# Twenty-eight products ahead of the first transposes, and the first weight load behind the first token tile, in a one-core hybrid encoder layer

## The reference

```python
def reference(x, w_in, ...):
    u = x @ w_in[l]                       # (1024, 1024) @ (1024, 7688)
    ua, ub, uc, ug = _split(u, GROUP_COLS)
    oa = _gdn_branch(ua, ...)             # gated DeltaNet
    ob, v_first = _rwkv7_branch(ub, ...)  # RWKV-7
    oc = _swa_branch(uc, sinks)           # sliding-window attention
    merged = (gates[:, :, 0] * (oa @ w_branch_a[l]) + gates[:, :, 1] * (ob @ w_branch_b[l])
              + gates[:, :, 2] * (oc @ w_branch_c[l]))
    x = _layer_norm(ALPHA * x + merged @ w_out[l], ln1_w[l], ln1_b[l])
    hid = jax.nn.silu(x @ ffn_gate[l]) * (x @ ffn_up[l])
    x = _layer_norm(ALPHA * x + hid @ ffn_down[l], ln2_w[l], ln2_b[l])
    return x
```

## Time and profile before

| what | us |
|---|---|
| median of three runs | 1816.58 |
| span of the profiled execution | 1816.2 |
| PE busy in it | 1781.5 (98%) |
| first transpose on PE | 6.35 |
| first product of the projection on PE | 13.42 |

### The profile page before, as it was taken

One profiled execution on the slowest core, in us unless ns is written; L12 is line 12 of the kernel. 1 busy time (PEld: TensorE's weight loads), 2 busy tenths in 40 slices (PEclk: granted clock), 3 DMA queues, 4 the chain that ended last, 5 costly groups with the idle time before them and its releaser, 6 DMA issues. The chain is left out here.

```text
span 1816.2 us, 28096 instructions
## 1 busy us (share of the span) xinstructions
PE 1781.5 (98%) x11148; PEld 1471.3 (81%) x11148; DVE 1141.4 (63%) x1354; ACT 665.2 (37%) x1126; POOL 584.6 (32%) x418
## 2 busy tenths in 40 slices
PE   8999999999999999999999999999999999999997
PEld 7778787777788888788878788888888888888886
DVE  2856665666419930377768854966666665665577
ACT  3534434244421211355542231343333333344341
POOL 1211222212213332344415452755455554500000
PEclk9999999999999999999999999999999999999999
DMA  6255575235673377377665573225545455488464
GB/s 178 50 112 140 141 180 138 65 76 155 166 206 93 93 162 228 126 237 245 186 211 173 163 236 97 101 70 183 171 133 171 143 175 179 139 286 300 169 226 155
DMA packets 386434, 293.24 MB, mean 161 GB/s; under 512 B 172428, under 2 KB 318412, under 8 KB 384256
## 3 DMA queue, kind: packets, MB, share of 16 engines
q1 hardware_dynamic: 310080, 237.63, 44.1%
q10 hardware_dynamic: 76224, 53.81, 10.3%
HBM read 196.33 MB, written 94.98 MB: 160 GB/s over the span
## 5 line engine op out<-in xcount | busy, mean ns | idle before, releaser
L168 PE MATMUL bank<-xhi,w_hi 128*128 128x512 f32 x960 | 379.0, 395 | 2.5 <-ACT turned L847 1.7
L170 PE MATMUL bank<-xhi,w_lo 128*128 128x512 f32 x960 | 374.4, 390 | 0.0
L169 PE MATMUL bank<-xlo,w_hi 128*128 128x512 f32 x960 | 373.8, 389 | 0.0
L472 POOL TENSOR_TENSOR w_lo<-w_raw,w_hi 128x1024 fp32r<-128x1024 f32 x59 | 168.3, 2853 | 538.1 <-ACT w_hi L854 538.1
L168 PEld LDWEIGHTS bank<-xhi,w_hi 128*128 128x128 f32 x960 | 180.3, 188 | 43.3 <-issue 6.8
L170 PEld LDWEIGHTS bank<-xhi,w_lo 128*128 128x128 f32 x960 | 180.2, 188 | 38.4
L169 PEld LDWEIGHTS bank<-xlo,w_hi 128*128 128x128 f32 x960 | 180.4, 188 | 36.1
L2044 POOL TENSOR_TENSOR ff_ring_lo<-ff_w_sums,ff_ring_hi 128x512 fp32r<-128x512 f32 x88 | 125.7, 1430 | 74.6 <-ACT ff_ring_hi L2326 74.4
L2044 POOL TENSOR_TENSOR ff_ring_lo<-ff_raw,ff_ring_hi 128x512 fp32r<-128x512 f32 x66 | 96.2, 1460 | 149.4 <-ACT ff_ring_hi L2326 149.4
L834 ACT ACTIVATE work<-bank 128x512 f32<-128x512 f32 x68 | 40.7, 598 | 244.7 <-PE bank L170 228.4
L175 PE MATMUL b_ps<-x1hi,ff_ring_hi 128*128 128x512 f32 x264 | 102.9, 390 | 0.0
(11 more groups left out here) (418 smaller groups left out, 3968.7 us busy)
## 6 DMA issues: line engine op xcount, KB each, us to landing
w_raw<-in_w_in ACTq DMA_DIRECT2D x61, 512.0 KB, 4.3
hid_ops<-y SPq DMA_DIRECT2D x77, 256.0 KB, 2.8
ff_raw<-hid_ops SPq DMA_DIRECT2D x77, 256.0 KB, 3.9
op<-opnd SPq DMA_DIRECT2D x16, 1152.0 KB, 5.5
u<-work ACTq DMA_DIRECT2D x68, 256.0 KB, 4.3
b_gate<-u SPq DMA_DIRECT2D x24, 512.0 KB, 3.6
ff_raw<-in_ffn_gate SPq DMA_DIRECT2D x22, 512.0 KB, 4.5
ff_raw<-in_ffn_up SPq DMA_DIRECT2D x22, 512.0 KB, 5.7
```

Of the source, the lines that this page charges most:

```text
L168: pe.matmul(out, w_hi, x_hi, start=first, stop=False)
L169: pe.matmul(out, w_hi, x_lo, start=False, stop=False)
L170: return pe.matmul(out, w_lo, x_hi, start=False, stop=last)
L472: pool.tensor_tensor(w_lo[b][:, :, :], w_raw[b][:, :, :], as_f32(w_hi[b][:, :, :]), ALU.subtract).then_inc(w_lo_done, 1)
```

## The change

POOL's first instruction becomes a clearing of 128 columns of slab 17, announced by a semaphore (the former `early_cleared`, renamed `early_zeroed`, whose later wait rises from 4 to 5 for it). PE waits for it and makes 28 products of this piece with itself, 128x128 by 128x128, into the first 128 columns of bank 3, before it waits for the constants; nothing reads the result, and the transposes overwrite it. And ACT waits for `x_landed[0]` before `load_w(0)`.

```diff
+IDLE_PRODUCTS = 28
...
         def _(pool):
+            pool.memset(work[:, 17, 0:P], 0.0).then_inc(early_zeroed, 1)
             pool.wait_ge(w_lo_done, 1)
...
-                pool.memset(inv[b][:, :, :, :], 0.0).then_inc(early_cleared, 1)
-                pool.memset(join[b][:, :, :], 0.0).then_inc(early_cleared, 1)
-            pool.wait_ge(early_cleared, 4)
+                pool.memset(inv[b][:, :, :, :], 0.0).then_inc(early_zeroed, 1)
+                pool.memset(join[b][:, :, :], 0.0).then_inc(early_zeroed, 1)
+            pool.wait_ge(early_zeroed, 5)
...
+            pe.wait_ge(early_zeroed, 1)
+            for _ in range(IDLE_PRODUCTS):
+                pe.matmul(bank[3][:, 0:P], work[:, 17, 0:P], work[:, 17, 0:P], start=True, stop=True)
             pe.wait_ge(const_landed, 16)
             for i in range(4):
                 pe.wait_ge(x_landed[i], 16)
...
+            act.wait_ge(x_landed[0], 16)
             load_w(0)
             split(0)
             load_w(1)
```

More of the change, by code:

```diff
@@ L419, in project_and_prepare @@
         inv_landed, inv_cleared, inv_stored = sem("inv_landed"), sem("inv_cleared"), sem("inv_stored")
-        early_landed, early_inv, early_cleared, early_join, early_placed = (sem("early_" + n) for n in ("landed", "inv", "cleared", "join", "placed"))
+        early_landed, early_inv, early_zeroed, early_join, early_placed = (sem("early_" + n) for n in ("landed", "inv", "zeroed", "join", "placed"))
         inv_step = [sem(f"inv_step{k}") for k in range(2)]
```

## The result

The changed kernel takes 1824.51 us, the median of six runs (1822.39 to 1829.24), against 1816.86 us of the kernel before on the same chips (six runs, 1814.23 to 1820.21). The ratio is 1.0044 with a 95% interval of 1.0032 to 1.0056: slower by 7.7 us (the two medians), with 1823.5 us forecast. The profiled executions differ by as much, 1823.7 against 1816.2 us of span.

A forecast was written before the change was run, and what follows sets the result against it. PE, busy 1781.5 of 1816.2 us, was taken as the bound. A late first product (+4.4 us) and low clock (+2.5) sum to +6.9: span 1823.1, forecast 1823.5 us with the median 0.4 above the span; range 1818.5 to 1827.

The forecast's parts named there:

- The path: At the kernel's start: the first weight load, issued at 4.7 us behind seven queued token tiles, lands about when these drain.
- The working by packets: Queues at the start: token and weight packets alternate, 98 token packets per us, putting the last weights at 14.3 us.
- The landing: First weight tile lands at 14.7 us, some 0.5 us behind its last bytes; bounds 13.5 and 17.
- From landing to product: From the weight tile's landing through split, lo part and first `xlo` to PE's first product: 3.15 us.
- The late first product: PE's first product starts at 17.85 us instead of 13.42: +4.4 us, bounds +3.2 and +6.7.
- The clock: After about 8 us idle, PE's first products run at the low clock: +2.5 us, bounds 1.6 and 3.2.
- The 28 products: At PE's start: they take 3.1 to 6.0 us, end between 4.2 and 7.1, and raise the clock for the transposes.
- A: Rival: weight load takes its median 4.3 us and lands at 9.0; 1815.4 us, or 1817.0 with low clock; chance 0.15.
- B: Rival: weights land late, but the clock stays up or later PE waits shrink; +3.5 us, 1820.1; chance 0.13.
- C: Rival: weights come early enough that tokens decide, first product 2.9 us sooner; 1813.7 us; chance 0.04.
- D: Rival: first token tile no sooner, weight load issued at 6.3 and landing at 17 us; +9.9, 1826.5; chance 0.08.
- the three that would have been wrong: Signs against the forecast: weight landing before 10.5 us, full pace from the first product, or weight load issued after 6 us.

The follow-up runs named there:

- the wait alone: Kernel before plus only ACT's wait for the first token tile ahead of the weight load, no clearing or products: 1826.55 us, ratio 1.0052.
- the parameters held: Changed kernel, but SP issues the small parameters only once the weight tile has landed, all eight token tiles still ahead: 1823.64 us, ratio 1.0043.
- 12 products: Changed kernel without ACT's wait (weight load first) and 12 full-size products instead of 28: 1815.56 us, ratio 0.9996; again 1815.40 us, 0.9992.
- 16 products: Changed kernel without ACT's wait (weight load first) and 16 full-size products instead of 28: 1812.64 us, ratio 0.9982; again 1812.37 us, 0.9972.
- the 28 products alone: Changed kernel without ACT's wait, so clearing and 28 products only, weight load first as before: 1817.55 us, ratio 1.0002.
- with 48: Whole changed kernel, ACT's wait included, with 48 products instead of 28: 1823.12 us, ratio 1.0038.
- 6 products: Changed kernel without ACT's wait (weight load first) and 6 products instead of 28: 1817.55 us, ratio 1.0006.
- the tiles held back: Changed kernel, but SP issues token tiles 4 to 7 and the parameters only once the weight tile has landed: 1820.43 us, ratio 1.0024.

## Why the prediction was right, point by point

**The path.** The step that decided, that the weight load would be slowed by seven token tiles queued before it and not by its late issue, held: 11.5 us to landing where I had 10.0 (14.7 - 4.7), and 5.8 with only three tiles and no parameters beside it. The working by packets has 360 token packets moved by 6 us, the tokens gone at 12.8 and the last weights at 14.3 us; it was 299 packets by 6 us, a little after 14, and 15.5. The weights' first packet came 3.8 us behind the issue, at 8.70 us (20 packets in all between 6 and 9 us).

**The landing.** I took 14.7 us and it was 16.4. Two terms were too small. The larger error is the time of the last packet, 14.3 in the sum and 15.5 measured; the other is the tail, 0.5 us assumed and 0.9 measured (0.45 when the parameters are held back). The second weight tile of the kernel before had shown such a tail, 1.1 us from its last packet at 16.4 to its landing at 17.5, and I had counted it among the packets.

**From landing to product**: 3.15 us in the sum; 19.53 - 16.47 = 3.06 measured. **The late first product** was thus +6.1 instead of +4.4, inside its bounds.

**The clock**: +2.5 in the sum, +1.4 measured, a little under its lower bound of 1.6; in the wait alone and with the parameters held it was what I took: the 24 products then last 2.9 and 2.5 us longer than before (6.1 and 5.4 us of them at 0.50). PE idle for 6.4 us and not 8, since the 28 products lasted longer, was not what shortened it: with the parameters held PE was idle 4.7 us and had the low clock for longer. What sets the length of the low clock stays open; the three profiles show 3.0, 5.4 and 6.1 us of products at it behind waits of 6.4, 4.7 and 8.9 us. The two errors, 1.7 too little and 1.1 too much, nearly cancel, and that the forecast came within about 1 us of the measured time is luck to that extent.

**The 28 products** were mis-sized by a factor of two. The trace has them as 56 passes of 0.215 and 0.107 us; they ended near 9.5 us and not between 4.2 and 7.1, and started the first transposes 3 us later than before (9.46 against 6.35). It cost nothing, as the weight tile was later still; alone it costs 0.9 us of start. Rows 11 could have told: the line that I took for 16 products is a loop over 8.

**Tile 0** landed at 4.9 us (4.6 forecast). **The rule on transposes** of the Trainium skill (TensorE: Matmul & The Clock Gate, PE-mode transpose), that the full clock doesn't engage for them: no trace here agrees. With 12 products eight of them go in 0.9 us when the tile is there, and in the wait alone they quicken with nothing but transposes before them.

**The span and the time.** I put the profiled execution 0.4 us under the median of the runs. The results give for each profiled run both numbers, 1823.7 of span and 1825.85 of device time for the changed kernel, so the distance is 2.15 us, and the profile of before was of an execution of some 1818.3 us, 1.6 above its median. For the difference it made nothing.

**The rivals.** A (a quick load) is out by 11.5 us to landing; B (made up later) by the later matmuls of PE, 7.5 us late at 222 us, at 623 us and at the end; C (full use of the quicker token path) by the late weights, and even with the weight load first 12 and 16 products gave 1.5 to 1.8 us of start where C had 2.9; D (tile 0 no sooner) by its landing at 4.9.

**The signs.** ACT's wait for that transfer, the low clock in the first products and fewer than 24 of them in 5.4 us came as named. Five others lay outside what I gave: the weight load was issued at 4.90 us (4.2 to 4.8), landed at 16.4 (13.5 to 15.5), the products ended near 9.5 (6 or 7), the transposes were done at 13.1 (10), and the first product came at 19.53 (17 to 19). None of the three that would have been wrong showed.

## What to carry to other kernels

A transfer that is moved behind others is priced by what stands in the queues when it is issued, not by its own size: with packets taken in turns, the one with rows of 512 bytes beside rows of 4096 got an eighth of the bytes here (0.15 of 1.24 MB from 9 to 12 us) until the other queue was empty. When two inputs meet, look which of them has time to spare and how much before delaying it (here 3.3 us of spare time against 9.5 us of delay). And before a gain of a microsecond or two is put down to an edit, add the same number of instructions with next to no work in them: here 16 such products were worth 2.8 us by themselves (ratio 0.9976 to 0.9996), and 12 nothing.

## What the runs showed of the hardware that I had not expected

A 128x128 product of full 32-bit floats is two passes, each as long as a transpose of that size: 0.43 us at the low clock, 0.215 to 0.22 at the high one (28 products, 56 rows, 8.4 us).

The clock rose at different distances from PE's first work in executions that begin alike: by the pace of its instructions, 3.0 and 3.7 us with 12 products, 3.8 and 4.2 with 16, 4.4 in the changed kernel, 5.4 with the 28 products alone and 6.2 with 48, where PE was busy from 1.0 us on in all seven; 5.6 us in the kernel before. With 6 products, which ended at 3.9 us and were followed by 2.4 us of nothing, it had not risen when the transposes began.

The landing of the 512 KB weight tile came 0.9 us behind its last packet in the changed kernel, 1.0 with the wait alone and 1.2 with 48 products, with 4-byte packets of the other queue under way each time, and 0.45 us with the parameters or the tiles held back, when there were none in those 0.45 us.

The position of PE's instructions in its program moves the time of the recurrences by some 3 us: 0.3 to 0.7 us of waits without a shown cause in 175 us with 16 products of either size (three executions), 3.3 to 5.9 with 12 (three), 4.1 in the kernel before. A wait of 2 us among them was followed by 3.4 us at the low clock with 12 small products.
